# A diffusion trunk step on one core: modulation columns summed by VectorE, ScalarE and GpSimd, with TensorE left for the last sum over partitions

## The reference

```python
m = jax.nn.silu(cond) @ w_ada + b_ada          # (2048) @ (2048, 6 * 2048)
sh1, sc1, g1, sh2, sc2, g2 = split(m, 6)
h = rmsnorm(x, norm1) * (1 + sc1) + sh1
q, k, v, u = h @ w_in                          # q, k RMS-normed per head
attn = context or 2-D neighbourhood attention  # 12 heads of 128
ssm  = S5 scans on u, gelu, GLU
x = x + g1 * (concat(attn, ssm) @ w_out)
h = rmsnorm(x, norm2) * (1 + sc2) + sh2
x = x + g2 * expert_choice_ffn(h)              # 16 experts, SwiGLU
```

## Time and profile before

| what | value |
|---|---|
| time of the runs shown | 2477.36, 2481.3 and 2487.31 us, median 2481.3 |
| profiled execution | its span is 2481.0 us, from its first to its last instruction; no other time is given for it |
| share of the span busy | TensorE 94%, VectorE 24%, ScalarE 14%, GpSimd 12% |
| heads, first to last projection matmul | 448.9 to 1069.9 us |
| chain that ended last, by engine | TensorE 76%, DMA 14%, VectorE 4%, issue 2%, ScalarE 2% |
| chain, the lines of the heads | L1315 14%, L1805 2%, L1343 2% (1.8% to one decimal), L1303 1%, L1328 1% |
| mean granted TensorE clock | 0.979 of full speed |

### The profile page before, as it was taken

How to read it: one execution, slowest core, us unless ns; L and a number is a source line. 1 busy time by engine, 2 the same in 40 slices (tenths; PEclk the granted TensorE clock), 3 DMA queues, 4 the chain that set the end, 5 groups by cost and what they waited for, 6 DMA issues and landing times.

```text
span 2481.0 us, 56996 instructions
## 1 busy us (share of the span) xinstructions
PE 2335.6 (94%) x26284; PEld 1515.0 (61%) x26284; DVE 593.2 (24%) x907; ACT 337.0 (14%) x771; POOL 285.7 (12%) x404
## 2 busy tenths in 40 slices
PE   5999999999999999999999489999999999999997
PEld 3468888555555556554445386666666666666663
DVE  4124332244444433421015600000000000000001
ACT  3011111022232232320002100000000000000000
POOL 1156760000000000000030100000000000000000
PEclk9999999999999999999999699999999999999999
DMA  9923114856555411224322778999999999999995
GB/s 372 353 69 91 56 47 84 277 183 223 198 181 194 153 57 46 89 95 152 145 88 117 286 304 365 409 409 409 408 411 409 411 411 410 407 403 408 405 404 195
DMA packets 181751, 628.75 MB, mean 253 GB/s; under 512 B 12778, under 2 KB 89284, under 8 KB 151108
## 3 DMA queue, kind: packets, MB, share of 16 engines
q1 hardware_dynamic: 163008, 585.04, 61.1%
q0 software_dynamic: 3328, 20.97, 3.2%
q10 hardware_dynamic: 15188, 19.19, 2.3%
HBM read 600.72 MB, written 24.44 MB: 252 GB/s over the span
## 4 chain that ended last, share of the span: by engine, by line
PE 76%; DMA 14%; DVE 4%; issue 2%; ACT 2%; SPq 1%; ACTq 1%; POOL 0%; DVEq 0%; POOLq 0%
PE PS L1496 18%; PE PS L1315 14%; PE PS L1406 11%; PE PS L1510 9%; DMA work<-in_w_gate 8%; PE PS L1131 7%; DMA hT_<-in_w_gate 4%; PE PS L1008 3%; PE PS L1073 3%; DVE work L1805 2%; PE PS L1343 2%; DMA work<-in_w_ada 1%; PE PS L1303 1%; PE PS L1035 1%; PE PS L1328 1%
## 5 line engine op out<-in xcount | busy, mean ns | idle before, releaser
L1496 PEld LDWEIGHTS PS<-hT_,work 128*64 128x64 f32 x14336 | 511.6, 140 | 90.0 <-issue 71.2
L1496 PE MATMUL PS<-hT_,work 128*64 128x80 f32 x14336 | 530.8, 235 | 32.1 <-issue 20.1
L1315 PE MATMUL PS<-hT_,work 128*128 128x512 f32 (+1 forms) x1536 | 442.3, 438 | 0.0
L1315 PEld LDWEIGHTS PS<-hT_,work 128*128 128x128 f32 x1536 | 225.3, 192 | 158.6 <-issue 158.5
L1510 PE MATMUL PS<-work,hT_ 128*32 128x512 f32 (+1 forms) x2544 | 301.7, 596 | 6.2 <-DMA work<-in_w_down 3.2
L1406 PE MATMUL PS<-work,mixT_ 128*128 128x512 f32 x640 | 279.5, 597 | 0.0
L1922 DVE TENSOR_TENSOR hT_<-PS,hT_ 128x480 f32<-128x480 f32 x16 | 10.5, 658 | 930.7 <-ACT hT_ L991 930.7
L1131 PE MATMUL PS<-work,hT_ 128*128 128x256 f32 x960 | 212.7, 380 | 0.9 <-DMA work<-in_w_in 0.9
L1406 PEld LDWEIGHTS PS<-work,mixT_ 128*128 128x128 f32 x640 | 121.7, 192 | 149.0 <-issue 149.0
L1131 PEld LDWEIGHTS PS<-work,hT_ 128*128 128x128 f32 x960 | 180.4, 190 | 26.4 <-DMA work<-in_w_in 1.3
L1510 PEld LDWEIGHTS PS<-work,hT_ 128*32 128x32 f32 (+1 forms) x2544 | 71.3, 105 | 150.7 <-issue 138.0
(11 more groups left out here) (255 smaller groups left out, 1776.9 us busy)
## 6 DMA issues: line engine op xcount, KB each, us to landing
work<-in_w_up SPq DMA_DIRECT2D x57, 2048.0 KB, 26.8
work<-in_w_down SPq DMA_DIRECT2D x56, 2048.0 KB, 32.3
work<-in_w_gate SPq DMA_DIRECT2D x55, 2048.0 KB, 31.3
work<-in_w_ada SPq DMA_DIRECT2D x48, 2048.0 KB, 13.1
work<-in_w_in SPq DMA_DIRECT2D x80, 512.0 KB, 4.9
hT_<-in_w_gate SPq DMA_DIRECT2D x9, 2048.0 KB, 34.3
work<-in_w_out SPq DMA_DIRECT2D x4, 4096.0 KB, 13.2
hT_<-in_w_down SPq DMA_DIRECT2D x8, 2048.0 KB, 31.0
```

The source lines that it names most:

```text
L1315: last = pe.matmul(bank(2 * which, n, col), w_chunk[chunk % NW][:, HD * (k % 8):HD * (k % 8) + HD], hT[:, k, col:col + n], start=(k == 0), ...
L1496: last = pe.matmul(hidden_at(u, f)[64 * h:64 * h + 64, :], w[:, k % 4, f // 2, f % 2, 64 * h:64 * h + 64], xsT[s][:, k, :], start=opens, s ...
```

## The change

The 16 pieces are multiplied with the conditions by other engines. Each piece has 16 slices of 128 rows by 512 columns, 256 slices in all, 24 in a step (`LATE_STEP`), so that they fill the steps 0 to 10.

- VectorE sums a piece for the latent condition: one `scalar_tensor_tensor` for each slice, slice times column of the condition plus the sum so far, which stands in PSUM bank 3 (`acc_bank`); the last one of a piece writes to SBUF (`acc_lat`). Each waits for the one before.
- ScalarE multiplies each slice with the context condition (Identity with a scale per partition) into one of three `prod` buffers, the first of a piece into `acc_ctx`, and GpSimd adds them up, 15 adds of 128 x 512 for a piece. ScalarE waits for the add of three products ago. Its program has the 24 products of a step in eight groups of three, next to the slots.
- TensorE's `late` is gone. `late_sums` has four matmuls of 512 columns with ones as weights for a pair of pieces, in four column groups of bank 4, eight pairs in all. One VectorE add (`late_rows`) takes the bias, now loaded into 128 partitions, in place of four.
- To free bank 3, q lies in bank 0 and a quarter of bank 1, and k in the last quarter of bank 1 and in bank 2, context first. The context part of k now waits for the normed q (`s_qn`).
- SyncE issues three halves in a step, not four, and each waits for VectorE and ScalarE to be through with the half two before.
- TensorE's latent part of k is cut 4:8 and 8:12 around slot 4, no longer 4:7, 7:9 and 9:12.
- Two semaphores are merged with others (`s_xss` with `s_nroot`, `s_finT` with `s_rawT`).

```diff
...
+LATE_PAIRS = 8
+LATE_STEP = 24
...
-        b_late = [take(512, 2) for _ in range(2)]
...
-        row_late = [take(512, 2) for _ in range(2)]
+        at(8256)
+        acc_lat = [take(BANK) for _ in range(2)]
+        acc_ctx = [take(BANK) for _ in range(3)]
+        prod = [take(BANK) for _ in range(3)]
+        at(12368)
+        row_late = [take(BANK)]
         assert used[0] <= 12880
+        at(heads_end)
+        row_late.append(take(BANK))
+        assert used[0] <= ring_at
...
+        acc_bank = bank(3)
...
-                p, x = n // 2, n % 2
+                p, x, j = n // 2, n % 2, n // 4
                 if n >= 2:
-                    sp.wait_ge(s_late_mm, n - 1)
-                cols = slice(2 * D + p * BANK, 2 * D + (p + 1) * BANK)
-                sp.dma_start(late_ring[x], w_ada_v[:, 8 * x:8 * x + 8, cols]).then_inc(s_late[x], 16)
-                if x == 0:
-                    if p >= 2:
-                        sp.wait_ge(s_late_row, p - 1)
-                    sp.dma_start(b_late[p % 2], t["b_ada"][:, cols].to_broadcast([2, BANK])).then_inc(s_late[0], 16)
+                    sp.wait_ge(s_lated, n - 1)
+                    sp.wait_ge(s_prod, 8 * (n - 1))
+                col = 2 * D + p * BANK
+                sp.dma_start(late_ring[x], w_ada_v[:, 8 * x:8 * x + 8, col:col + BANK]).then_inc(s_late[x], 16)
+                if n % 4 == 0:
+                    if j >= 2:
+                        sp.wait_ge(s_late_out[j % 2], 32 * (j // 2))
+                    for i in range(2):
+                        sp.dma_start(row_late[j % 2][64 * i:64 * i + 64],
+                                     t["b_ada"][:, col + i * BANK:col + (i + 1) * BANK].to_broadcast([64, BANK]))\
+                            .then_inc(s_late[0], 16)
...
-                if h < 8:
-                    late(4 * h + 2)
-                    late(4 * h + 3)
+                if 3 * h + 2 < 32:
+                    late(3 * h + 2)
...
+                rows = pairs_by(h, bool(which))
+                if rows:
+                    pe.wait_ge(s_late_row, rows)
+                pe.matmul(bank(4), ones, sq[which][:, lat_at[which]], start=True, stop=True)
+                pe.matmul(ctx_sums(which), ones, sq[which][:, ctx_at[which]], start=True, stop=True).then_inc(s_ss, 1)
+
+            def late_sums(h, end):
+
+                for j in range(LATE_PAIRS):
+                    if summed_in(j) == (h, end):
+                        pe.wait_ge(s_lated, 4 * j + 4)
+                        pe.wait_ge(s_padd, 30 * j + 30)
+                        pe.wait_ge(s_root, 2 * h + end)
+                        for i in range(2):
+                            pe.matmul(bank(4)[64 * i:64 * i + 32, :], ones[:, 0:32], acc_ctx[(2 * j + i) % 3], start=True, stop=True)
+                            last = pe.matmul(bank(4)[64 * i + 32:64 * i + 64, :], ones[:, 0:32], acc_lat[i], start=True, stop=True)
+                        last.then_inc(s_late_mm, 1)
...
                 part(h, 0, False, range(0, 2))
                 if g >= 0:
                     sums(g, 1)
-                part(h, 0, False, range(2, 6))
-                if h < 8:
-                    late(4 * h)
-                part(h, 0, False, range(6, 8))
-                if h < 8:
-                    late(4 * h + 1)
+                part(h, 0, False, range(2, 8))
+                late_sums(h, False)
                 part(h, 0, False, range(8, 12))
                 slot(g, 0)
                 if g >= 0:
@@ -1383,15 +1440,11 @@
                 context_key(h)
                 part(h, 1, False, range(3, 4))
                 slot(g, 3)
-                part(h, 1, False, range(4, 7))
-                if h < 8:
-                    late(4 * h + 2)
-                part(h, 1, False, range(7, 9))
+                part(h, 1, False, range(4, 8))
                 slot(g, 4)
-                if h < 8:
-                    late(4 * h + 3)
-                part(h, 1, False, range(9, 12))
+                part(h, 1, False, range(8, 12))
                 slot(g, 5)
+                late_sums(h, True)
                 part(h, 1, False, range(12, 16))
                 slot(g, 6)
                 part(h, 1, True, range(16))
...
+                STT(dst[h % 2], qk_bank(which), gain, rstd, ALU.mult, ALU.mult).then_inc(done, 1)
+
+            def late_rows(h, end):
+
+                for j in range(LATE_PAIRS):
+                    if summed_in(j) == (h, end):
+                        dve.wait_ge(s_late_mm, j + 1)
+                        TT_(row_late[j % 2], bank(4), row_late[j % 2], ALU.add).then_inc(s_late_row, 1)
+
+            def late(h, first, n):
+
+                for m in range(LATE_STEP * h + first, min(LATE_STEP * h + first + n, 16 * 16)):
+                    p, k = m // 16, m % 16
+                    if k % 8 == 0:
+                        dve.wait_ge(s_late[k // 8], late_landed(p, k // 8))
+                    w, c = late_ring[k // 8][:, k % 8, :], cTv[:, 1, k:k + 1]
+                    if k == 0:
+                        ch.link(TS_(acc_bank, w, c, None, ALU.mult))
+                    elif k == 7:
+                        STT(acc_bank, w, c, acc_bank, ALU.mult, ALU.add).then_inc(s_lated, 1)
+                        dve.wait_ge(s_lated, 2 * p + 1)
+                    elif k == 15:
+                        if p >= 2:
+                            dve.wait_ge(s_late_mm, p // 2)
+                        STT(acc_lat[p % 2], w, c, acc_bank, ALU.mult, ALU.add).then_inc(s_lated, 1)
+                        dve.wait_ge(s_lated, 2 * p + 2)
+                    else:
+                        ch.link(STT(acc_bank, w, c, acc_bank, ALU.mult, ALU.add))
 
             def step(h):
                 g = h - 1
                 if g >= 0:
                     normed(g, 1)
-                if h < 8:
-                    late_row(2 * h)
+                late_rows(h, False)
+                late(h, 0, 3)
                 for k in range(3):
                     slot(g, k)
+                    late(h, 3 + 3 * k, 3)
                 if h < HEADS:
                     normed(h, 0)
+                late(h, 12, 2)
                 for k in range(3, 6):
                     slot(g, k)
-                if h < 8:
-                    late_row(2 * h + 1)
+                    late(h, 14 + 3 * (k - 3), 3)
+                late_rows(h, True)
                 slot(g, 6)
+                late(h, 23, 1)
 
...
```

More of the change, by code:

```diff
@@ L429, in used_up_to, with summed_in, pairs_by, late_landed @@
             return r + 1 if r < 8 else r - (r - 8) % 12 + USED[(r - 8) % 12] + 1
+        def summed_in(j):
+            m = 32 * j + 31
+            return (m // LATE_STEP, True) if m % LATE_STEP < 16 else (m // LATE_STEP + 1, False)
+        def pairs_by(h, end):
+            return sum(summed_in(j) <= (h, end) for j in range(LATE_PAIRS))
+        def late_landed(p, x):
+            return 16 * (p + 1) + (0 if x else 32 * (p // 2 + 1))
         def done_gate_up(e):
@@ L682, in _ @@
                 act.activation(small[:, 24 + tiles[0]:25 + tiles[-1]], small[:, 16 + tiles[0]:17 + tiles[-1]], ACT.Sqrt,
-                               bias=eps[:, :], scale=1 / D).then_inc(s_xss, 1)
+                               bias=eps[:, :], scale=1 / D).then_inc(s_nroot, 1)
             for i in (3, 4):
@@ L892, in squares @@
                     act.wait_ge(s_ss, 2 * h + which - 1)
-                act.activation(sq[which], bank(2 * which, TOK), ACT.Square).then_inc(s_sq, 1)
+                act.activation(sq[which], qk_bank(which), ACT.Square).then_inc(s_sq, 1)
             def root(h, which):
@@ L900, in root @@
                     act.wait_ge(s_kn, h)
-                act.activation(rstd[:, 0:N_LAT], bank(4), ACT.Sqrt, bias=eps[:, :], scale=1 / HD)
-                act.activation(rstd[:, N_LAT:TOK], bank(2 * which + 1, P, P), ACT.Sqrt, bias=eps[:, :], scale=1 / HD)\
+                act.activation(rstd[:, lat_at[which]], bank(4), ACT.Sqrt, bias=eps[:, :], scale=1 / HD)
+                act.activation(rstd[:, ctx_at[which]], ctx_sums(which), ACT.Sqrt, bias=eps[:, :], scale=1 / HD)\
                     .then_inc(s_root, 1)
@@ L933, in step @@
                 slot(g, 2)
+                late(h, 9, 3)
                 if h < HEADS:
@@ L1310, in part @@
                     pe.wait_ge(s_vev, 7 * TT if ctx_ else 7 * TT - 1)
+                if which and ctx_:
+                    pe.wait_ge(s_qn, h + 1)
                 for k in ks:
@@ L1314, in part @@
                         landed_chunk(chunk)
-                    last = pe.matmul(bank(2 * which, n, col), w_chunk[chunk % NW][:, HD * (k % 8):HD * (k % 8) + HD],
+                    last = pe.matmul(qk_bank(which)[:, (ctx_at if ctx_ else lat_at)[which]], w_chunk[chunk % NW][:, HD * (k % 8):HD * (k % 8) + HD],
                                      hT[:, k, col:col + n], start=(k == 0), stop=(k == KT - 1))
@@ L2049, in _, with late, bias @@
                     phases(m + 1)
-            pool.wait_ge(s_span, 256)
```

(18 more changed lines are left out.)

102 lines of the change are left out of this document (52 added, 50 removed).

## The result

The changed kernel takes 2491.15 us (median of 8 runs, 2485.34 to 2492.39), the kernel before 2483.34 beside it (8 runs, 2477.36 to 2487.31). The ratio is 1.0027, with a 95% interval from 1.0017 to 1.0037: no change within 0.5%, as forecast, and 7 us above the predicted 2484. The profiled execution took 2492.05 us, with a span of 2490.3.

A forecast was written before the change was run, and what follows sets the result against it. A chain from key copy through root, reciprocal, bias and exponential sets slot 4's start. Ten steps +5.0, last sums +7.6, step 11's cut +0.9, start -11.0 give +2.5, rounded to +3 on 2481.0: 2484 us, range 2467 to 2508.

The forecast's parts named there:

- TensorE's calls go: Up to the sums of step 1, six `late` calls of 1.84 us vanish from TensorE: 11.0 us gained.
- VectorE's two sums ahead of slot 3: Two added sums between the normed q and slot 3's bias lie on the chain: +1.55 us a step.
- ScalarE's three products: Products ahead of the key copy, with slot 2 later, delay the root: +0.7 us a step, bounds 0 and 1.3.
- The new cut: One matmul of k's latent part moves behind slot 4, onto the path: +0.86 us a step.
- The clock: TensorE's half-speed stretch behind its longer wait at slot 4: +0.2 us a step, bounds -1.0 and +1.7.
- The last sums: TensorE's four overlapping matmuls for each pair of pieces: 0.95 us each, eight times, 7.6 us in all.
- GpSimd and the loads: GpSimd's adds keep up and three halves a step stay hidden: cost 0, for GpSimd at most 3 us once.
- rival 1: GpSimd's adds hold up VectorE's reciprocal or scaling around slot 3, 1.27 us each a step: 2497 or 2510 us; chance 0.22.
- rival 2: Loads or GpSimd's pace set the step in the heads, some 2 us a step: 2504 us; chance 0.08.
- rival 3: In the steps, ScalarE's products fit and the slow clock vanishes in the longer wait: 2465 us; chance 0.16.
- rival 4: TensorE's new sums in the heads don't overlap and cost as much as `late`, 20 us more: 2504 us; chance 0.04.

The follow-up runs named there:

- filled wait: Five matmuls with unread results put into TensorE's wait ahead of slot 4 in steps 1 to 10 of the changed kernel: 2468.29 us, ratio 0.9939.

## Why the prediction was right in its verdict and short in its size

By its own steps:

- **TensorE's calls go**, -11.0 at the start: measured -13.3, since a call costs 2.03 among other matmuls and not 1.84, and a wait of 1.05 for w_ada went with them. 8.1 of it lie between `sums(0, 0)` and `sums(1, 0)` (40.39 in place of 48.50).
- **VectorE's two sums ahead of slot 3**, +1.55: right. 1.54 to 1.58 in the trace, 1.58 when they are taken away and 1.60 when they are doubled.
- **ScalarE's three products**, +0.7: the root comes 0.43 later. The way was right in part, products in a gap that a late slot 2 makes too small, but GpSimd's hold on slot 1's scaling is needed for it, and that I had only as a rival of 1.27 or nothing. The upper bound of 1.3 doesn't come out of its own working, which gives 1.0 to 1.2.
- **The new cut**, +0.86: right; the wait changes by 0.86, and the ten steps by 8.6 without the clock's share.
- **The clock**, +0.2 with bounds -1.0 and +1.7: this is the step that failed in size. The ten steps less the eight sums (539.06 - 8.7, at 1.09 each) are 53.0 each, 3.6 over 49.46; S to slot 4 is 1.96 of it on average and the cut 0.86, which leaves 0.7 to 0.8. The filled wait bears it out. The slow clock costs 2.2 us in a step now. Before, it cost 1.5: at full clock, in the filled kernel's step without a sum over partitions, it is 38.1 from slot 4 to the next `sums`, less the moved 0.86 is 37.2, and the kernel before took 38.7. So 0.5 more a step than forecast, about 5 us of the forecast's shortfall in ten.
- **The last sums**, 0.95 each: 1.09 in the timeline (963.41, when the next matmul could have begun, to 964.50), +1.1 in all. In the filled kernel a step with a sum is 1.2 longer behind slot 4 than one without, so it may be +2.
- **GpSimd and the loads**, 0: right for this kernel. 31.4 us busy in a step, ScalarE waits 8.4 us in all for it, w_ada lands in 9.7 us (13.1 before). It holds only while products are spread; with six in a row GpSimd's pace ends last.

So TensorE was relieved of 7.4 us a step, and the steps got 0.1 shorter than with `late`, 53.9 for 54.05, because slot 4 hangs on a chain through ScalarE and VectorE. The work was cover for that chain; taken away, TensorE waits 5.1 us in its place and pays for the wait with its clock. By terms, the heads' forecast was +2.5 and the outcome +4.3: 3.8 more in the steps, 0.3 more in step 11, and 2.3 saved at the start. The rest of the difference, 5.0 us of span, lies ahead of the heads, where the experiments show it to be chance, and behind them, where it stays open; executions of the changed kernel spread over 7 us (2485.34 to 2492.39).

The rivals: GpSimd's hold is real, but 0.3 us a step where 1.0 would decide (rival 1). Under another order it was 0.86, with TensorE waiting behind it. The reciprocal ahead of slot 3 was never held: 4.15 in all 24 cases, in the step shown with adds of GpSimd beside it from 947.82 to 951.78. In steps 1 to 10 neither VectorE nor ScalarE waited for w_ada, and TensorE waited for neither GpSimd nor the loads (rival 2). The products and the clock did not both fall well (rival 3), and the sums do overlap (rival 4).

## What to carry to other kernels

Work taken off the busiest engine gains only where that engine ends last; here it had to be followed by bringing other work of its own into the wait (the cut) and by clearing the chain that it waits for (VectorE's sums, ScalarE's table load, GpSimd's adds beside VectorE's scaling). The unchanged amount of work, in another order, is worth 56 us. When filler moves to other engines, place each piece by what stands behind it in the queue: an idle engine's average says nothing of the 1.5 us in which it is on the chain. And a fixed buffer count couples producer and consumer: as many pieces as there are buffers go at the producer's pace, the next ones at the consumer's.

## What the runs showed of the hardware

- Fifty unread matmuls made the kernel 22.9 us faster. Behind a wait of TensorE its granted clock falls to 0.50, 1.2 in place of 2.4 GHz, and the loss in a step is not in proportion: 10 us from slot 4 have a mean clock of 1.00 after a wait of 0.82 (filled), 0.83 after 2.23 (before), 0.73 after 5.1, 0.79 after 6.7. After 2.10 it was 0.66 to 1.00 and after 1.23 it was 0.83 or 1.00, in steps of one execution each. What decides between these is left open; I measured the cost and not its rule.
- A 128x384 scaling of VectorE between SBUF tiles takes 0.42 us alone, 0.74 to 1.28 when one of GpSimd's adds of 1.27 is under way at its start, and it ends 0.2 behind that add (937.97 for 937.75, 925.38 for 925.16). A reciprocal of 128x640 between SBUF tiles, begun at 947.17 beside an add that ran until 947.54, kept its 4.15. The sums with one operand in PSUM kept their 0.74 to 0.76 all the time, with GpSimd at 60% of the step.
- ScalarE's product of 128x512 with a scale for each partition is 0.71 us alone, and three in a row 1.94: each behind the first costs 0.61.
